# Five landing places for the down-projection's weights, and the last residual of three token tiles added in memory

## The reference, cut to what matters

```python
h = rms_norm(x, norm_ffn_pre[l]) * (1.0 + sc2) + sh2
y = conv_glu_ffn(h, w_up[l], conv_w[l], conv_b[l], w_down[l])   # ends in (gelu(a) * b) @ w_down
x = x + g2 * rms_norm(y, norm_ffn_post[l])
```

## Time and profile before

| | |
|---|---|
| median of 3 runs | 2429.55 us (2429.44 to 2430.79) |
| the profiled execution, its own time | 2431.21 us |
| span of its trace | 2429.4 us |
| TensorE matmul busy | 2313.9 us, 95% of the span |
| VectorE busy | 1887.9 us, 78% |
| ScalarE busy | 1103.1 us, 45% |
| GpSimd busy | 111.3 us, 5% |
| chain that ended last | PE 82%, DVE 7%, DMA 6%, ACT 2%, issue 2%, SPq 1% |

### The profile page before, as it was taken

One profiled execution on the slowest core, in us unless ns is written; L12 is line 12 of the kernel. 1 busy time (PEld: TensorE's weight loads), 2 busy tenths in 40 slices (PEclk: granted clock), 3 DMA queues, 4 the chain that ended last, 5 costly groups with the idle time before them and its releaser, 6 DMA issues.

```text
span 2429.4 us, 36942 instructions
## 1 busy us (share of the span) xinstructions
PE 2313.9 (95%) x13613; PEld 2032.6 (84%) x13613; DVE 1887.9 (78%) x2416; ACT 1103.1 (45%) x1495; POOL 111.3 (5%) x185
## 2 busy tenths in 40 slices
PE   2899999999999999989999999999999989999996
PEld 2777778888888878868999999999999967788875
DVE  6965667787777763267899999999999967889888
ACT  5356743333333342264444444444444434554553
POOL 1010000000000000000000000000000000000000
PEclk9899999999999999989999999999999999999998
DMA  9952456676666525235655555555555477655564
GB/s 371 336 143 71 143 174 215 200 240 210 209 206 215 190 70 183 95 121 144 174 143 145 143 143 143 144 142 143 142 142 143 108 241 255 231 182 198 186 255 156
DMA packets 371311, 430.90 MB, mean 177 GB/s; under 512 B 14268, under 2 KB 291012, under 8 KB 368928
## 3 DMA queue, kind: packets, MB, share of 16 engines
q1 hardware_dynamic: 354704, 369.74, 47.8%
q0 software_dynamic: 16528, 60.15, 10.2%
HBM read 407.27 MB, written 54.54 MB: 190 GB/s over the span
## 4 chain that ended last, share of the span: by engine, by line
PE 82%; DVE 7%; DMA 6%; ACT 2%; issue 2%; SPq 1%; DVEq 0%; ACTq 0%
PE bank L1973 24%; PE bank L1974 24%; PE bank L1975 24%; DMA DRAW<-in_w_down_dram 3%; PE bank L2130 2%; DVE W_lo L1842 2%; DMA W_raw<-t_dram 2%; DMA ADA<-in_w_ada_dram 1%; PE bank L2039 1%; PE bank L2162 1%; DVE ACC L1305 1%; DVE GS_lo L1839 1%; PE bank L2149 1%; DVE DRAW L1820 1%; PE bank L2030 1%
## 5 line engine op out<-in xcount | busy, mean ns | idle before, releaser
L1973 PE MATMUL bank<-H_lo,W_hi 128*128 128x256 f32 (+1 forms) x1888 | 660.3, 350 | 3.3 <-DVE H_lo L1320 3.3
L1975 PE MATMUL bank<-H_hi,W_lo 128*128 128x256 f32 (+1 forms) x1888 | 635.8, 337 | 0.0
L1974 PE MATMUL bank<-H_hi,W_hi 128*128 128x256 f32 (+1 forms) x1888 | 635.6, 337 | 0.0
L1973 PEld LDWEIGHTS bank<-H_lo,W_hi 128*128 128x128 f32 x1888 | 360.3, 191 | 42.7 <-issue 7.7
L1974 PEld LDWEIGHTS bank<-H_hi,W_hi 128*128 128x128 f32 x1888 | 360.3, 191 | 39.5 <-issue 7.7
L1975 PEld LDWEIGHTS bank<-H_hi,W_lo 128*128 128x128 f32 x1888 | 359.6, 190 | 37.9
L1973 PE MATMUL bank<-T_lo,W_hi 128*128 128x256 f32 x1280 | 362.2, 283 | 0.0
L1974 PE MATMUL bank<-MGR,W_hi 128*128 128x256 f32 x1280 | 362.2, 283 | 0.0
L1975 PE MATMUL bank<-MGR,W_lo 128*128 128x256 f32 x1280 | 362.2, 283 | 0.0
L1973 PE MATMUL bank<-W_lo,GS_hi 128*128 128x512 f32 x616 | 243.6, 395 | 20.1 <-DVE W_lo L1842 20.0
L1259 DVE TENSOR_TENSOR W_lo<-W_raw,W_hi 128x1024 fp32r<-128x1024 f32 x138 | 168.3, 1220 | 104.7 <-ACT W_hi L709 104.3
(11 more groups left out here) (279 smaller groups left out, 3618.9 us busy)
## 6 DMA issues: line engine op xcount, KB each, us to landing
AB_raw<-in_w_ada_dram SPq DMA_DIRECT2D x128, 512.0 KB, 4.5
UB<-in_w_up_dram SPq DMA_DIRECT2D x100, 512.0 KB, 4.1
W_raw<-in_w_in_dram SPq DMA_DIRECT2D x90, 512.0 KB, 4.7
t_dram<-in_w_down_dram POOLq DMA_DIRECT2D x66, 512.0 KB, 7.6
W_raw<-in_w_up_dram SPq DMA_DIRECT2D x56, 512.0 KB, 4.0
W_raw<-in_w_down_dram SPq DMA_DIRECT2D x56, 512.0 KB, 4.2
DRAW<-in_w_down_dram SPq DMA_DIRECT2D x54, 512.0 KB, 4.1
ADA<-in_w_ada_dram SPq DMA_DIRECT2D x32, 512.0 KB, 5.7
```

Of the source, the lines that this page charges most:

```text
L1973: pe.matmul(acc, st_hi, mv_lo, start=start, stop=False)
L1974: pe.matmul(acc, st_hi, mv_hi, start=False, stop=False)
L1975: return pe.matmul(acc, st_lo, mv_hi, start=False, stop=stop)
```

## The change

Four things are edited. (1) A fifth landing place, `DRAW[4]`, and a load waits for the low part of the unit five before it, not for a whole couple; where that unit's weight is also the first term of a sum that comes later, it waits for the sum too. (2) The wait at `load_g` is for the couple two earlier, with four semaphores in turn. (3) `GROW2` is loaded at the start of sweep 1. (4) The end: the last three couples of sweep 3 are ordered by e, then m; the residual of tiles 0 to 2 is copied from `x1_dram` to `out` in memory early in sweep 3, ScalarE scales `YG` of these tiles by the inverse root, and GpSimd adds the result onto `out` by accumulating transfers of 1 MiB. Only tile 3 is finished by VectorE and stored by SyncE as before.

```diff
-DOWN[-3], DOWN[-2] = DOWN[-2], DOWN[-3]
+DOWN[-6:] = sorted(DOWN[-6:], key=lambda unit: (unit[2], unit[1]))
+DOWN_RAW = 5
...
-            W_raw[:, 0, :], W_raw[:, 1, :]]
+            W_raw[:, 0, :], W_raw[:, 1, :], at("DRAW4", [P, 1024], F32, 60 * KB)[:, :]]
...
                 elif d < SLOTS:
-                    sp.wait_ge(lo_ready, U_DOWN - 1)
...
-                    sp.wait_ge(lo_ready, U_DOWN + partner(d - SLOTS) + 1)
+                elif d < DOWN_RAW:
+                    sp.wait_ge(unit_used, U_DOWN)
+                else:
+                    before = d - DOWN_RAW
+                    sp.wait_ge(lo_ready, U_DOWN + before + 1)
+                    if partner(before) > before:
+                        sp.wait_ge(sum_ready, 2 * (FT - PLAIN) + W_SUMS[partner(before) + 1])
...
-                    sp.wait_ge(gs_hi, DOWN.index((0, m, 0)) + 1)
+                    if m >= 2:
+                        sp.wait_ge(gs_hi, DOWN.index((0, m - 2, 0)) + 1)
                     load_g(m + 2)
...
-            pool.wait_ge(unit_used, U_DOWN)
+            pool.wait_ge(unit_used, U_DOWN + SWEEP_AT[1])
             pool.dma_start(GROW2[:, :], gate_dram[1:2, :].partition_broadcast(P)).then_inc(grow_landed, 16)
-            pool.wait_ge(gs_lo, SWEEP_AT[3] + KT)
             pool.wait_ge(x1_stored, 16 * TT)
-            for tt in range(TT):
-                pool.dma_start(X1[:, tt, :], x1_dram[tt * P:(tt + 1) * P, :]).then_inc(x1_landed, 16)
+            pool.wait_ge(unit_used, U_DOWN + SWEEP_AT[3] + 4)
+            for tt in range(TT - 1):
+                pool.dma_start(out[0, tt * P:(tt + 1) * P, :], x1_dram[tt * P:(tt + 1) * P, :]).then_inc(x1_landed, 16)
+            pool.wait_ge(gs_lo, SWEEP_AT[3] + 8 * TT)
+            pool.dma_start(X1[:, TT - 1, :], x1_dram[(TT - 1) * P:TT * P, :]).then_inc(x1_landed, 16)
+            pool.wait_ge(x1_landed, 16 * TT)
+            for tt in range(TT - 1):
+                pool.wait_ge(y_scaled, tt + 1)
+                pool.dma_start(out[0, tt * P:(tt + 1) * P, :], YG[:, tt, :], accum_op=ALU.add).then_inc(y_added, 16)
...
+            def scale_y(tt):
+                act.wait_ge(y_done, tt + 1)
+                act.wait_ge(yg_ready, 8 + 2 * (tt + 1))
+                act.activation(YG[:, tt, :], YG[:, tt, :], ACT.Copy, scale=col(SM, RSY + tt)).then_inc(y_scaled, 1)
+            for b in range(8):
+                last_square(b)
+                if b in (3, 5):
+                    y_root(b // 2 - 1)
+                    scale_y(b // 2 - 1)
+            y_root(TT - 2)
+            y_root(TT - 1)
+            scale_y(TT - 2)
...
+                if d == len(DOWN) - 1:
+                    last_sums(0, (0, 1))
+                    gate_y(0, (0, 1))
                 down_low(d)
...
+            for tt in range(1, TT - 1):
+                last_sums(tt, (2 * tt, 2 * tt + 1))
+                gate_y(tt, (2 * tt, 2 * tt + 1))
+                finish(tt - 1)
+            last_sums(TT - 1, (6,))
+            gate_y(TT - 1, (6,))
+            last_sums(TT - 1, (7,))
+            finish(TT - 2)
+            finish(TT - 1, (7,))
...
+            last_banks((d0 + 3, d0 + 4), 0, (0, 1)).then_inc(y_tile_done, 1)
+            last_banks((d0 + 3, d0 + 4), 1, (0, 1), True).then_inc(y_tile_done, 1)
+            down_unit(d0 + 5, (d0 + 5) % 4, 4, False, False)
+            last_banks((d0 + 6, d0 + 7), 2, (0, 1)).then_inc(y_tile_done, 1)
+            last_banks((d0 + 6, d0 + 7), 3, (0,)).then_inc(y_tile_done, 1)
+            last_banks((d0 + 6, d0 + 7), 3, (1,)).then_inc(unit_used, 1)
```

More of the change, by code:

```diff
@@ L338, in hybrid_encoder_layer @@
         sum_ready, n1_kept, posted = sem("sum_ready"), sem("n1_kept"), sem("posted")
-        g_stored, g_landed = [sem(f"g_stored{e}") for e in range(2)], [sem(f"g_landed{k}") for k in range(2)]
-        t2_landed, down_landed = sem("t2_landed"), [sem(f"down_landed{k}") for k in range(2)]
+        g_stored = [sem(f"g_stored{e}") for e in range(2)]
+        t2_landed, y_scaled, y_added = sem("t2_landed"), sem("y_scaled"), sem("y_added")
+        assert KT == 2 * ADA1_SLOTS
+        g_landed, down_landed, ada1_count = ada1_landed[0:4], ada1_landed[4:7], 2 * 16
         gs_hi, gs_lo, yg_ready, y_squared, y_rms, y_done = (
@@ L391, in down_raw @@
         def down_raw(d):
[L393 to L395 removed]
+            place, n = d % DOWN_RAW, d // DOWN_RAW + 1
+            if place in (2, 3):
+                return raw_landed[place - 2], 16 * (U_ST // 2 + n)
+            return down_landed[min(place, 2)], ada1_count + 16 * n
         def by_tile(row):
@@ L1915, in _, with finish @@
                         last_step(n)
-            for tt in range(TT):
-                banks = (6,) if tt == TT - 1 else (2 * tt, 2 * tt + 1)
-                last_sums(tt, banks)
-                gate_y(tt, banks)
-                if tt == TT - 1:
-                    last_sums(tt, (7,))
+            def finish(tt, banks=()):
                 dve.wait_ge(y_squared, 8 + 2 * (tt + 1))
                 dve.tensor_reduce(col(SM, RSY + tt), SM[:, SSY + 4 * tt:SSY + 4 * tt + 4], AX.X, ALU.add).then_inc(y_summed, 1)
-                if tt == TT - 1:
-                    gate_y(tt, (7,))
+                gate_y(tt, banks)
                 dve.wait_ge(y_rms, tt + 1)
+                if tt < TT - 1:
+                    dve.reciprocal(col(SM, RSY + tt), col(SM, RSY + tt)).then_inc(y_done, 1)
+                    return
                 after(dve.reciprocal(col(SM, RSY + tt), col(SM, RSY + tt)))
@@ L2419, in _, with last_banks @@
                         down_unit(d, d % 4, 4 if d % 2 else 0, False, d >= SWEEP_AT[3] - 2)
-            d0 = len(DOWN) - 4
-            for tt in range(TT - 1):
-                for d in (d0 + 2 * (tt // 2), d0 + 2 * (tt // 2) + 1):
-                    down_ready(d)
-                    for b in (2 * (tt % 2), 2 * (tt % 2) + 1):
-                        ins = down_bank(d % 4, b, b + 4 * (tt // 2), False, d % 2 == 1)
-                ins.then_inc(y_tile_done, 1)
-            for d in (d0 + 2, d0 + 3):
-                ins = down_bank(d % 4, 2, 6, False, d % 2 == 1)
-            ins.then_inc(y_tile_done, 1)
-            for d in (d0 + 2, d0 + 3):
-                down_bank(d % 4, 3, 7, False, d % 2 == 1).then_inc(unit_used, 1)
+            d0 = len(DOWN) - 8
+            for d in range(d0, d0 + 3):
+                down_unit(d, d % 4, 4 if DOWN[d][2] else 0, False, False)
+            def last_banks(units, tt, bs, told=False):
+                for d in units:
+                    down_ready(d)
+                    for b in bs:
+                        ins = down_bank(d % 4, 2 * (tt % 2) + b, 2 * tt + b, False, d == units[-1])
+                    if told and d == units[0]:
+                        ins.then_inc(unit_used, 1)
+                return ins
+            last_banks((d0 + 3, d0 + 4), 0, (0, 1)).then_inc(y_tile_done, 1)
[4 more added lines that the diff above has]
+            last_banks((d0 + 6, d0 + 7), 3, (1,)).then_inc(unit_used, 1)
 _INS = ['x', 'c', 'w_ada', 'b_ada', 'norm_mix_pre', 'norm_mix_post', 'w_in', 'q_norm', 'k_norm',
```

58 lines of the change are left out of this document (25 added, 33 removed).

## The result

The changed kernel takes 2413.35 us (median of 4 runs, 2410.83 to 2415.20), the kernel before beside it 2430.17 (4 runs, 2429.44 to 2433.48). The ratio is 0.9927, with a 95% interval of 0.991 to 0.9945. The profiled execution of the changed kernel has an own time of 2410.83 us and a span of 2408.7.

The account below looks back on a forecast made before the run. TensorE, 95% busy, bounds; only stalls and the tail can shrink. 2431.21 - 25.8 (4.16 + 10.45 + 10.07 + 2.12 - 1.0) + 0.9 = 2406.3, less 1.66 to the median: 2404.5 said, range 2397 to 2412.

Parts of the forecast that it names:

- the loop of sweep 0: Down-projection units 9 to 43: with earlier loads into five places, all 10.07 us lost there go.
- Rival B: Sweep 0 becomes bound by the transfers; half of the 10.07 us stays, giving 2408.5; chance 0.17.
- The 1.0 us put back for imperfect overlap: Units 9 to 43: 1.0 us held back from the 10.07 us gain (bounds 0 and 10.07).
- The start: Units 0 to 8: 4.16 us of waiting go in units 0 to 3 and 10.45 us in 4 to 8.
- The collision in sweep 3: Units 127 and 128, beside X1 loads: earlier weight loads save TensorE 2.12 us (bounds 2.12 gained, 3 lost).
- The accumulates' price: Tail: each 1 MiB accumulate takes 5.4 us of the engines, 3.1 issue and completion; span ends E + 23.2.
- E: The moment TensorE's last matmul ends, from which the tail's times are counted; 2407.1 in the kernel before.
- a last store near E + 14: Tail: sign that VectorE's last store of tile 3 lands at E + 14.2, before the span's end.
- Rival A: Tail: accumulates run at the plain rate, tail ends at E + 15.7, time 2398; chance 0.15.
- D: Tail: accumulates do not overlap, 20.4 us each; ends E + 62.5, slower than before at about 2444; chance 0.02.
- What ends the span: Tail: the third accumulate ends last, E + 23.2 against E + 22.3 before, costing 0.9 us more.
- Rival C: Copies or accumulates bite: 3 us stay at the copies, accumulates take 6.6 us each; 2413; chance 0.08.

Follow-up runs that it names:

- e8: The kernel before with one edit, GROW2 loaded at the start of sweep 1: 2427.33 us, ratio 0.9991.
- e2: The kernel before with the changed loading alone (five places, new waits, GROW2 in sweep 1), old unit order, X1 loads and tail: 2403.88 us, ratio 0.9885.
- e5: The changed kernel without copies, scalings or accumulates; VectorE adds all four tiles and SyncE stores them: 2405.56 us, ratio 0.9894.
- e7: The changed kernel with each copy made in two halves of 1024 columns, rows of 4 KiB instead of 64: 2413.54 us, ratio 0.9926.
- e4: The changed kernel with plain stores in place of the accumulates, leaving out the residual of tiles 0 to 2: 2405.52 us, ratio 0.9894.
- e3: e2 with the last 512 columns of tile 3 stored by GpSimd's queue instead of SyncE's: 2410.78 us, ratio 0.9912.
- e11: e6 run again beside e12 on one chip: 2401.64 us, ratio 0.9878.
- e1: The changed kernel run again, unedited: 2412.36 us, ratio 0.992 to the kernel before.
- e12: e2 run again beside e11 on one chip: 2405.83 us, ratio 0.9886.
- e6: e5 with tile 0 alone copied, scaled by ScalarE and accumulated; tiles 1 to 3 stay with VectorE: 2404.09 us, ratio 0.9891.
- e10: e2 with four landing places instead of five, loads still waiting for single units: 2411.03 us, ratio 0.9911.

## Why the prediction was right, and where it was wrong

The time came out 8.8 us above the forecast and above the range. Two steps of the prediction failed in what they said of the kernel: the path behind the last accumulate, where GpSimd's drain lies (3.5 us of tail instead of 0.9), and the wait in sweep 3, which was to give back 2.12 us and still cost 1.96. A third was no step at all: the stages ahead of the down-projection stood in the sum at nothing, since no edit touches them, and the largest part of the miss lies there, as far as the profiles can tell.

**What bounds, and the loop of sweep 0: right.** The stretch of 44 units was to take 122 to 124 us and takes 122.27. The DMA share is 0.86 at 290 GB/s (0.84 and 289 forecast), the landing 5.4 (4.5 to 6.5), and from 2000 on no engine waits for a landing there. Rival B, a loop bound by the transfers, falls. The 1.0 us put back for imperfect overlap was hardly needed: units 4 to 43 took 0.15 over their 108.80.

**The start: right in size, half right in reason.** Units 0 to 3 came out at 13.32, as reckoned, and the 10.45 us of units 4 to 8 went. But the prediction gave the move of `GROW2` as the first reason for the latter, and e8 shows that this move alone takes units 4 to 8 only from 24.05 to 21.05 us. The other 7.45 needed loads that leave earlier.

**The collision in sweep 3: wrong, "a landing of 12.1 us no longer reaches TensorE: 2.12 us go".** With `X1` loads it is true (e2, e5: no wait in sweep 3). With copies of 64 KiB rows a weight lands after 13.0, and 1.96 us stay, inside the bound of 3 us lost that was named and not taken. e7 takes the wait away with smaller rows in more transfers. TensorE's end came 24.25 us earlier on the span's clock and not 25.8: 1.96 stayed, the first matmul came 0.44 later, 0.85 of the 1.0 us held back was not needed.

**The accumulates' price: right.** 0.731 x 16 x 22 / 3.15 = 81.7 us of an engine per MB, 5.35 us of all sixteen for 1 MiB; 5.4 was taken. Their sum with tile 3's stores was to end at E + 23.2 and did at E + 22.3. Only the sign given for it was wrong, a last store near E + 14: the stores are slowed by the accumulates beside them and land last. Rival A (the plain rate) falls by e4's 7.2 us of difference, and D (20.4 us each) by landings of 7.8 to 12.2. By its own terms A's time is 2404.6 - 0.9 - 6.6 = 2397.1, not 2398.

**What ends the span: wrong, "what ends last is the third accumulate".** GpSimd's drain ends 4.16 us behind it, at E + 25.6. The tail costs 3.5 us and not 0.9. The prediction read the tail of a kernel whose last transfer on that queue was issued 108 us before the end, where the drain is over long before the last store. It priced every step that the views of before show; the drain stands in none of them, though its record is in that trace, 4.05 us behind the last `X1` load's landing. e3 shows it with one small store, and e11 how it is hidden again.

**The stages ahead: the largest part of the miss, and not in the sum.** The forecast is a difference of 24.9 us laid on the median of before, 2429.55. The profiled execution of before stood 1.66 us above its median, and the changed kernel's was the fastest of its four runs, 2.52 below. These four, each with the mean granted clock of its trace:

| us | 2410.83 | 2412.61 | 2414.08 | 2415.20 |
|---|---|---|---|---|
| clock | 0.988 | 0.987 | 0.986 | 0.986 |

The down-projection and the tail repeat to 0.15 us between profiles of one kernel (after and e1, e2 and e12, e6 and e11), while the first matmul of the down-projection lies anywhere from 1957.99 to 1963.99 us in the 14 profiles of this study. So the scatter comes from stages that no edit touches. A part of it can be placed. Behind a wait of TensorE of 2.1 to 2.2 us that ends between 908 and 913, which all 14 profiles have, the granted clock is 1.2 GHz for 3.4 us in eight of them (e3, e5 to e10 and e12), and not in the other six. The eight begin the down-projection at 1961.22 to 1963.99, the six at 1957.99 to 1960.95.

It is more than scatter around the same middle, and the rival that the profile does not show what the runs do holds so far. Profiles of down and tail together gain 21.2 us from before to after (470.48 to 449.25), the medians 16.8. In all 13 rows, after and e1 to e12, the median gains less than that part of the profile: e2 and e8 to e12 by 0.2 to 1.6 us, after, e1 and e3 to e7 by 2.3 to 6.9. e6 and e11 are the same kernel and fall short by 5.3 and 0.6, so the edits alone do not decide it.

The miss in terms of the sum: 1.55 (TensorE's end) + 2.56 (the tail) + 0.40 (outside the span, 2.18 against 1.78 us) + 4.18 (2.52 + 1.66, profile to median, which is where the stages ahead come in) + 0.1 (the forecast rounded down) = 8.8. Rival C came nearest, with 2413 and a chance of 0.08, but by accumulates of 6.6 us that were not so slow: its number was right by a price that stood for the drain.

**Open.** Why down and tail give 5.4 us between e1 and e2 in the profiles and 8.5 in the medians; what decides whether the clock falls near 910 us, and what makes up the rest of the earlier stages' differences; and what the drain does in its 4.2 us. In every profile it begins with the issue of GpSimd's last transfer, so no run shows what it would take if GpSimd itself first waited for the landing.

## What to carry to other kernels

When a change puts the last transfer of a kernel on another queue, price what the program does behind that queue's last landing, which a trace with an early last transfer hides; here the new order with one early accumulate gave 4.2 us of tail, and with three it took back 3.5. When loads wait in groups for groups, let each wait for its own release before adding buffers: that, with the activations' loads released earlier, gave 19.7 us here, the fifth buffer 4.0. And judge a change to one stage by that stage in the profiles, which repeated to 0.15 us here: the medians fell short of it by up to 6.9 us, and a range that is to hold for a median needs room for the stages that no edit touches.

## What the runs showed of the hardware

- GpSimd's closing drain ends 4.05 to 4.3 us after the last transfer of its queue has landed, in all 14 profiles: 2336.93 to 2340.98 (before), 2404.26 to 2408.42 (after), 2398.92 to 2403.07 (e4), 2407.8 to 2411.87 (e3), 2389.3 to 2393.35 (e11). The transfers were of 1 MiB and 256 KiB, loads and stores, accumulating and plain.
- An accumulating transfer of 1 MiB onto memory occupies the engines 5.35 us (after; a plain one 0.383 x 20 / 3 = 2.6 us, by e4's view), lands after 7.8 (after) and 8.1 us (e11) with none ahead of it and after 12.2 as the last of three, where plain ones land after 4.1 to 5.0 (e4).
- Stores of 256 KiB of another queue that share the engines with accumulates land after 11.8 us (after) and beside plain stores after 3.7 (e4).
- A copy memory to memory made in 64 KiB rows had a 512 KiB load land after 13.0 us beside it and TensorE lose 1.96 (after); in 4 KiB rows and six transfers the same load landed after 9.1 and no wait of TensorE was left (e7).
- Behind one and the same wait of TensorE near 910 us, of 2.1 to 2.2 us, the granted clock fell to 1.2 GHz for 3.4 us in eight profiles of 14 and stayed at 2.4 in six.
